# Turning the rotated queries and keys by a DMA trip and 32x32 block transposes instead of TensorE transposes

## The reference, cut to what matters

```
qa, ka, va = split(h @ w_in)          # 8 heads x 128, for moba; qb, kb, vb for dsa
ya = _moba_attention(_rope(qa), _rope(ka), va)
yb = _dsa_attention(_rope(qb), _rope(kb), vb, q_idx, k_idx, w_idx)

def _rope(x):                          # per head, half = 64
    x1, x2 = x[..., :half], x[..., half:]
    return concatenate([x1 * cos - x2 * sin, x2 * cos + x1 * sin])
```

## Time and profile before

| what | value |
|---|---|
| median of 3 runs | 1786.08 us (1785.97 to 1788.33) |
| the profiled execution's own time | 1786.64 us |
| its span, first to last instruction | 1785.0 us |
| PE busy | 1769.9 us, 99% of the span |
| DVE busy | 1259.2 us, 71% |
| ACT busy | 895.0 us, 50% |
| DMA, mean over the span | 250 GB/s, 446.93 MB |
| granted TensorE clock, mean | 0.999 |

### The profile page before, as it was taken

The page is one execution under the profiler, slowest core; times in us unless marked ns, Lnnn a source line. Parts: engine busy times, 40 slices in busy tenths (PEclk is TensorE's granted clock), DMA queues, the critical chain, the costliest instruction groups (busy, mean ns, idle before and its releaser), DMA issues.

```text
span 1785.0 us, 25525 instructions
## 1 busy us (share of the span) xinstructions
PE 1769.9 (99%) x8242; PEld 1454.6 (81%) x8242; DVE 1259.2 (71%) x1691; ACT 895.0 (50%) x1267; POOL 124.1 (7%) x217
## 2 busy tenths in 40 slices
PE   8999999999999999999999999999999999999998
PEld 7777778887888888888888888888888888888886
DVE  5677779778877867787777868777775654545545
ACT  6866675555445454544444545444444444444443
POOL 1011101010000000110010101000000000000000
PEclk9999999999999999999999999999999999999999
DMA  9778788655667778699999966999998775655554
GB/s 348 253 262 283 240 278 313 203 183 181 205 214 253 237 221 286 204 317 318 304 305 303 317 211 224 327 311 318 311 293 240 235 222 191 196 190 194 193 190 140
DMA packets 195053, 446.93 MB, mean 250 GB/s; under 512 B 17088, under 2 KB 27312, under 8 KB 194608
## 3 DMA queue, kind: packets, MB, share of 16 engines
q1 hardware_dynamic: 166544, 342.23, 58.9%
q0 software_dynamic: 28304, 103.89, 17.4%
q10 hardware_dynamic: 144, 0.03, 0.0%
HBM read 434.03 MB, written 12.06 MB: 250 GB/s over the span
## 4 chain that ended last, share of the span: by engine, by line
PE 95%; DMA 2%; DVE 1%; ACT 1%; SPq 0%; issue 0%; DVEq 0%; ACTq 0%
PE bank L1579 30%; PE bank L1581 30%; PE bank L1580 30%; DMA raw<-in_w_in_a 2%; PE bank L1625 1%; PE bank L1749 1%; PE bank L1732 1%; DVE w_lo L1001 0%; PE bank L1724 0%; PE bank L1842 0%; PE bank L1848 0%; PE bank L1721 0%; DVE x L1028 0%; PE bank L1605 0%; ACT y L594 0%; PE bank L1854 0%
## 5 line engine op out<-in xcount | busy, mean ns | idle before, releaser
L1001 DVE TENSOR_TENSOR w_lo<-raw,w_hi 128x1024 fp32r<-128x1024 f32 x605 | 728.8, 1210 | 412.2 <-ACT w_hi L590 409.9
L590 ACT ACTIVATE w_hi<-raw 128x1024 fp32r<-128x1024 f32 x605 | 633.5, 1050 | 712.0 <-PE bank L1581 644.1
L1579 PE MATMUL bank<-w_hi,h_hi 128*128 128x512 f32 x2272 | 896.2, 394 | 3.7 <-DVE w_lo L1001 2.4
L1581 PE MATMUL bank<-w_hi,h_lo 128*128 128x512 f32 x2272 | 885.8, 390 | 0.0
L1580 PE MATMUL bank<-w_lo,h_hi 128*128 128x512 f32 x2272 | 885.1, 390 | 0.0
L1579 PEld LDWEIGHTS bank<-w_hi,h_hi 128*128 128x128 f32 x2272 | 426.9, 188 | 95.8 <-issue 5.3
L1581 PEld LDWEIGHTS bank<-w_hi,h_lo 128*128 128x128 f32 x2272 | 426.6, 188 | 89.8
L1580 PEld LDWEIGHTS bank<-w_lo,h_hi 128*128 128x128 f32 x2272 | 427.1, 188 | 85.2
L515 POOL DMA_DIRECT2D ada_raw<-in_w_ada x160 | 84.7, 530 | 953.1 <-DVE acc_a L1008 709.8
L1008 DVE SCALAR_TENSOR_TENSOR acc_a<-ada_raw,cond,acc_a 128x1024 f32<-128x1024 f32 x112 | 143.3, 1280 | 10.8 <-DMA ada_raw<-in_w_ada 10.7
L1008 DVE SCALAR_TENSOR_TENSOR acc_b<-ada_raw,cond,acc_b 128x1024 f32<-128x1024 f32 x48 | 64.3, 1340 | 1.5 <-DMA ada_raw<-in_w_ada 1.4
(11 more groups left out here) (209 smaller groups left out, 934.6 us busy)
## 6 DMA issues: line engine op xcount, KB each, us to landing
raw<-in_w_ff SPq DMA_DIRECT2D x256, 512.0 KB, 4.7
raw<-in_w_in SPq DMA_DIRECT2D x176, 512.0 KB, 4.6
ada_raw<-in_w_ada POOLq DMA_DIRECT2D x160, 512.0 KB, 5.5
raw<-in_w_in_a SPq DMA_DIRECT2D x69, 512.0 KB, 5.0
ada_more<-in_w_ada POOLq DMA_DIRECT2D x32, 512.0 KB, 5.7
raw<-in_w_out_a SPq DMA_DIRECT2D x32, 512.0 KB, 5.6
raw<-in_w_o SPq DMA_DIRECT2D x32, 512.0 KB, 5.2
raw<-in_w_moba SPq DMA_DIRECT2D x16, 512.0 KB, 5.6
```

The lines of the kernel that those rows point to most:

```text
L590: act.activation(used(w_hi, turn, s), used(raw, turn, s), ACT.Copy).then_inc(hi_ready, 1)
L1001: dve.tensor_tensor(used(w_lo, turn, s), used(raw, turn, s), used(w_hi, turn, s).bitcast(F32), ALU.subtract).then_inc(lo_ready, 1)
L1579: pe.matmul(out_ap, hi, rhs_hi, start=start, stop=False)
L1581: return pe.matmul(out_ap, lo, rhs_hi, start=False, stop=stop)
```

## The change

The 64 PE transposes and the 16 ACT copies go. The rotation writes its result in another order of columns: for each quarter of the head dimension (32 wide) the two token halves and the four heads stand together, 256 columns or 1 KB. SP writes this block to DRAM in one DMA of 512 KB (`write_rot`, after the load of unit 6 of the K or V turn, once the rotation is done), and reads it back in four DMAs of 128 KB in rows of 1 KB (`read_rot`, after the load of unit 2 of the next turn, once the write has landed). Each read brings one quarter of the head dimension for all 128 tokens of a half to 32 partitions. The block lands in `rope_ab`, which is the space of `rope_a` and `rope_b`. DVE then transposes 32x32 blocks out of it into `q2_t` or `k2_t` (`turn_qk`, two instructions of 128x512 elements), at the end of its step s = 6 of the K or V turn. The next rotation waits until these two are done. The SP loop over the groups is written out, since the trips stand at fixed places in it. PE's `attn2` waits for the same count of `qk_ready` as before.

```
-                rope_a = sb("rope_a", [P, CH], on=a2)
-                rope_b = sb("rope_b", [P, CH], on=a2)
+                rope_ab = sb("rope_ab", [P, T * CH], on=a2)
...
+        rope_a, rope_b = rope_ab[:, 0:CH], rope_ab[:, CH:2 * CH]
+        rot_flat = rot[:, :, :].rearrange("p t n -> p (t n)")
+        rot_home = nc.dram_tensor("rot_home", (HEADS_2, P, T * CH), F32, kind="Internal").ap()
...
+            def write_rot(n):
+                sp.wait_ge(rot_ready, (n + 4) * T)
+                sp.dma_start(rot_home[n], rot_flat).then_inc(rot_written, 16)
+            def read_rot(n):
+                homes = rot_home[n].rearrange("(i r) (j n) -> j r i n", i=QUADS, j=QUADS)
+                sp.wait_ge(rot_written, (n + 1) * 16)
+                if n:
+                    sp.wait_ge(qk_ready, n * T)
+                for j in range(QUADS):
+                    sp.dma_start(rope_ab[j * QUAD:(j + 1) * QUAD, :].rearrange("p (i n) -> p i n", i=QUADS), homes[j])\
+                        .then_inc(rot_loaded, 16)
+            def load_with_rot(turn, col, written=None, read=None):
+                for s in range(UPT):
+                    load(turn, s, w_2[:, KG * s:KG * s + KG, col:col + CH])
+                    if s == UPT - 2 and written is not None:
+                        write_rot(written)
+                    if s == 2 and read is not None:
+                        read_rot(read)
+            for g in range(4):
+                for part in range(3):
+                    load_with_rot(g * 3 + TURN_GRP + part, g % 2 * CH + (g // 2 * 3 + part) * W2,
+                                  (None, 2 * g, 2 * g + 1)[part], (2 * g - 1 if g else None, None, 2 * g)[part])
+            load_with_rot(TURN_GATE, COL_GA, None, 7)
...
-            def keep_qk(n, dst):
-                for t in range(T):
-                    act.wait_ge(qk_turned, n * T + t + 1)
-                    act.activation(dst[:, :, t * P:t * P + P], two(banks[TURNED + t][:, :], 4), ACT.Copy)\
-                        .then_inc(qk_ready, 1)
...
+            rot_by_quad = rot_flat.rearrange("p (r e t h d) -> p t r h e d", r=2, e=2, t=T, h=4)
             def rope_chunk(p, turn, use, n):
                 for t in range(T):
                     chunk_result(t, turn, turn)
-                    rope(pair[p][t][:, :], rot[:, t, :], evicted[p][t], use, t, n, 4, DH_2 // 2, C_COS, C_SIN)
+                    rope(pair[p][t][:, :], lambda c, r: rot_by_quad[:, t, r], evicted[p][t], use, t, n, 4, DH_2 // 2,
+                         C_COS, C_SIN)
+            back = rope_ab[:, :].rearrange("p (i t h d) -> p t h i d", i=QUADS, t=T, h=4)
+            def turn_qk(g, n, dst):
+                dve.wait_ge(rot_loaded, g * (2 * 16 * QUADS) + (n + 1) * 16 * QUADS)
+                for t in range(T):
+                    dve.transpose(dst[:, :, t * P:(t + 1) * P], back[:, t]).then_inc(qk_ready, 1)
...
-                    dve.wait_ge(qk_turned, g * 2 * T)
+                    dve.wait_ge(qk_ready, g * 2 * T)
                 rope_chunk(PAIR_B, g * 3 + TURN_GRP, g * 2 + 7, g * 2 + 3)
                 for s in range(UPT):
                     split(g * 3 + TURN_GRP + 1, s + AHEAD)
...
+                    if s == 6:
+                        turn_qk(g, 0, q2_t)
-                dve.wait_ge(qk_turned, g * 2 * T + T)
+                dve.wait_ge(qk_ready, g * 2 * T + T)
                 rope_chunk(PAIR_A, g * 3 + TURN_GRP + 1, g + 9, g * 2 + 4)
...
+                    if s == 6:
+                        turn_qk(g, 1, k2_t)
...
-            def turn_qk(n):
-                for t in range(T):
-                    pe.wait_ge(rot_ready, (n + 3) * T + t + 1)
-                    turn_rows(rot, t, 4, banks[TURNED + t], qk_turned)
...
             def group_rest(g):
                 for s in range(UPT):
                     chunk_unit(g * 3 + TURN_GRP + 1, s, PAIR_A, g + 9)
-                    if s == 3:
-                        pe.wait_ge(o2_kept, g * 4 + 1)
-                        turn_qk(g * 2)
                 for s in range(UPT):
                     chunk_unit(g * 3 + TURN_GRP + 2, s, PAIR_B, g * 2 + 8)
-                    if s == 3:
-                        turn_qk(g * 2 + 1)
```

More of the change, by code:

```diff
@@ L297, in two_block_kernel @@
         mask_ready = sem("mask_ready")
-        qk_turned = sem("qk_turned")
+        rot_written = sem("rot_written")
+        rot_loaded = sem("rot_loaded")
         qk_ready = sem("qk_ready")
@@ L873, in group_rest @@
                     split(g * 3 + TURN_GRP + 1, s + AHEAD)
-                    if s == 4:
-                        keep_qk(g * 2, q2_t)
                 for s in range(UPT):
                     split(g * 3 + TURN_GRP + 2, s + AHEAD)
-                    if s == 4:
-                        keep_qk(g * 2 + 1, k2_t)
                 for t in range(T):
@@ L1292, in _, with rope @@
             residual_turn(1, TURN_QI - 1, PAIR_A, (7, 6), y1)
-            def rope(src, dst, stepped, use, t, n, heads, half, cos0, sin0, copies=1):
+            def rope(src, rows, stepped, use, t, n, heads, half, cos0, sin0, copies=1):
                 cols = heads * 2 * half
@@ L1309, in rope @@
                 dve.wait_ge(stepped, use + 1)
-                rows = dst.rearrange("p (h r d) -> p h r d", h=heads * copies, r=2)
                 for c in range(copies):
                     for r in range(2):
-                        ins = dve.tensor_tensor(rows[:, c * heads:(c + 1) * heads, r, :], ra[:, :, r, :], rb[:, :, r, :],
-                                                (ALU.subtract, ALU.add)[r])
+                        ins = dve.tensor_tensor(rows(c, r), ra[:, :, r, :], rb[:, :, r, :], (ALU.subtract, ALU.add)[r])
                 ins.then_inc(rot_ready, 1)
@@ L1338, in rope_index @@
                 chunk_result(t, turn, turn)
-                rope(pair[PAIR_A][t][:, :], rot[:, t, :], evicted[PAIR_A][t], 7 + n // 2, t, n, CH // IDX_DIM,
+                rows = rot[:, t, :].rearrange("p (h r d) -> p h r d", h=CH // IDX_DIM, r=2)
+                rope(pair[PAIR_A][t][:, :], lambda c, r: rows[:, :, r, :], evicted[PAIR_A][t], 7 + n // 2, t, n, CH // IDX_DIM,
                      IDX_DIM // 2, C_COSI, C_SINI)
@@ L1349, in _ @@
                     .then_inc(w_idx_ready, 1)
-                rope(ki[:, 0:IDX_DIM], rot_key[:, t, :], ki_roped, t, t, 1, 1, IDX_DIM // 2, C_COSI, C_SINI, 2)
+                rows = rot_key[:, t, :].rearrange("p (h r d) -> p h r d", h=2, r=2)
+                rope(ki[:, 0:IDX_DIM], lambda c, r: rows[:, c:c + 1, r, :], ki_roped, t, t, 1, 1, IDX_DIM // 2, C_COSI,
+                     C_SINI, 2)
             dve.wait_ge(i_turned, T)
```

## The result

The changed kernel takes 1790.85 us (median of 7 runs, 1788.65 to 1796.36) against 1786.08 us of the kernel before in the same session (7 runs, 1784.6 to 1788.33): a ratio of 1.003, 95% interval 1.0018 to 1.0041. It is slower by 0.3%; 1780.3 us was predicted, and the result lies above the range, which ended at 1786.5. The profiled execution took 1792.86 us with a span of 1790.8, 5.8 us longer than the span of before.

A forecast was written before the change was run, and what follows sets the result against it. PE's instruction stream (busy 99%) was taken as the bound. 7.04 us gained less 1.2 us lost (3 x 0.35 + 0.15) is 5.8 us, giving 1780.3 us against the median; range 1778.5 to 1786.5 us.

The forecast's parts named there:

- What is removed: 64 transposes in eight `turn_qk` steps leave PE's stream, 0.88 us a step on the chain: 7.04 us gained.
- rival 3: All the gain stays: the read lands in 5.5 us, before DVE comes; 1779.0 us; within the forecast's 0.63.
- DVE's block transposes: Two 32x32-block transposes per step on DVE, 0.7 us each, fitting exactly into a hole that is idle now.
- The write: Write of the rotated block to DRAM lands in 5.2 to 6.7 us and holds up nothing.
- The read's start: In group 1 the read back starts at 527.2 us, behind the load of V turn's unit 2.
- The slack: Time by which `w_lo` of V turn's unit 3 precedes PE's need: 1.6 us, 1.4 us in group 0.
- The read's length: Four reads, first issue to last landing: 8.6 us taken (5.5 best, 10.3 worst); PE loses 0.1 us.
- The queue: Queue shared with the four weight loads around the trip: mean loss of 0.35 us in each of groups 1 to 3.
- The keys' trip: Keys' trip one turn later, over 5 us of cover before PE wants `w_lo` and `k2_t`: costed at nothing.
- rival 1: Load queue too full from 524 us on, gain half eaten: 1782.5 to 1789.6 us; chance 0.22.
- rival 2: Write takes 9.1 us, DVE waits for a late read in K turns: 18.5 us lost, 1797.5 us; chance 0.12.
- Rival 4: A later stage that waits for DMA gives the 7 us back: 1786 us; chance 0.03.

## Why the prediction was wrong, step by step

- *What is removed: right.* 8 x 0.88 = 7.04 us was predicted; the run without the trip gained 6.8 (1779.4 us, where rival 3 said 1779.0), and 7.07 in the groups alone.
- *DVE's block transposes: right.* 0.7 us predicted, 0.69 measured; they fit the idle hole.
- *The write: too long.* 5.2 to 6.7 us taken from f's writes, 2.7 in group 1. It moved nothing: the read waits for its place behind a load in SP's order, as said. The estimate by the Trainium skill, "DMA: Bandwidth & Descriptors", section "Anatomy of one DMA", 3.2 us, was nearer here than the rows that I used; the page fits it to DMAs that GpSimd issues, and this one is SP's.
- *The read's start: right.* 527.2 predicted, 530.30 measured, in a run that stood 3.1 us later there (DVE's `w_lo` ends at 535.97 + 1.23 = 537.2 against 534.1).
- *The slack: about right.* 1.6 us (1.4 in group 0) was predicted. DVE's waits less PE's idle are 3.06 - 1.24 = 1.8, 2.75 - 0.68 = 2.1, 3.88 - 2.79 = 1.1 and 3.56 - 1.49 = 2.1 us.
- *The read's length: the step that failed.* "so I take 8.6" gave X = 1.7, the time by which the read lands after DVE asks for it. The reads took 8.8, 9.65, 11.8 and 10.5 us, DVE waited 3.06, 2.75, 3.88 and 3.56, and PE lost 6.2 us where 1.2 was summed. The rows of f and y had the same bad form, so their time was no price of 512 KB but of 512 KB into neighbours, in whatever queue stood around; here the mean is 10.2 us, as long as the worst of them (10.3). With the read in a good form the forecast of 1780.3 us comes true: 1781.01 us with the reorder on the way out, 1780.25 with the one read in rows of 4 KB. I saw the 0.97 share and did not ask what the same share moves.
- *The queue: priced far too low, the second step that failed.* For the four weight loads around the trip the sum has 0.35 us in each of three groups, 1.05 us. The run with traffic and no wait puts the traffic at 6.8 us in all, 5.6 of it in the groups.
- *The keys' trip: "I cost it at nothing" failed in group 0.* The prediction gave the keys over 5 us of cover. In group 0 DVE waited 2.43 us and then had no idle time to catch up with, since the masks are made in the same turn (DVE idles 0.5 us from 488.88 to 499.2), and PE waited 2.6 us for `s`. In groups 1 to 3 the keys' waits, 2.76 to 3.71 us, left no such wait of PE for `s`, so the cover held.
- *The clock: not foreseen.* 1.7 us, after PE's longest pause.

By size, in the profiled executions: 5.0 us for the queries' reads (6.2 against 1.2), 2.6 for the keys of group 0, 1.7 for the clock. The traffic's part is in these figures: late loads and DVE's wait hold up the same `w_lo`.

Of the rivals, rival 1 was the nearest: it named the full queue, and its worst case, X = 3.4 us and 7 us lost, is what the queries' trips did (3.3 us in the mean, 6.2 lost). That alone is no change, as it says; the keys' trip of group 0 and the clock made it slower, which is rival 2's outcome but not its way, since the write did not take 9.1 us. Rival 4, the time that comes back later, cannot be read from the changed kernel, which is not ahead after the groups (5.5 to 5.8 us behind to its end). In the runs that are ahead a small part of it is true: without the trip PE waits once near 1031 us, where before it did not,

```profile
1031.29 0.47 PE L1599 MATMUL bank<-w_hi,h_hi 128*128 128x512 f32 x1 [0.79 <-DVE w_lo L1009]
```

and 1.1 us of the gain are given back there, 1.4 us with the reorder on the way out.

## What to carry to other kernels

Let the DMA that goes through a full queue run over all 128 partitions in plain order, or over partitions spread among them; where the reorder must go by quarters of neighbours, put that side of the trip into the stretch whose queue is empty. Reaching all partitions is not enough by itself: the read cut by pieces of the row reached them all and was the slowest, with a source of only four entries outermost. Read a DMA share together with the GB/s beside it: a share of 1.0 at 290 GB/s can hide a transfer that holds the others up. A transfer's duration taken from another place of the kernel carries that place's form and queue with it; look for the same bytes in another form before using it as a price.

## What the runs showed of the hardware that was not expected

- By the packet records, which the views only sum, the median 4 KB packet of the reads took 159 ns into spread partitions or all 128, in each of the eight trips, and 228 to 303 ns into 32 or 64 neighbours, in all but two of sixteen trips (169 and 173 ns).
- The four neighbour DMAs as writes out of the memory, in the quiet stretch, cost little: all four done within 2.4 to 2.7 us of the first packet, where the one plain write of the changed kernel took 1.4 us, in one trip 2.1. What they cost in a full queue was not measured.
- Reads whose source has an outermost dimension of four entries left a DMA share of 0.26 behind them, a quarter of the engines with work, and cost 36 us over eight trips (1826.62 against 1790.85 us).
- A pause of 2.79 us of PE was followed by about 3 us at half clock; after the pause of 2.60 us in group 0 the clock stayed at 1.00. The length of the pause does not tell which: in the run with the reads two loads earlier the clock fell after a pause of 1.82 us (544.85 us), and with the reads on ScalarE's queue it stayed at 1.00 after one of 2.97 us (623.43 us).
